# Moving weights by 512 columns instead of x by 256 in the FFNs and output projections of a four-layer float32 trunk

## What is computed

```python
for i in range(DEPTH):
    x = x + 0.5 * _swiglu(_rms_norm(x, norm_ffn1[i]), ffn1_w_gate[i], ffn1_w_up[i], ffn1_w_down[i])
    h = _rms_norm(x, norm_mix[i])
    ...          # y = fox mixer, conv module or diff mixer of h, each with an output projection
    x = x + y
    x = x + 0.5 * _swiglu(_rms_norm(x, norm_ffn2[i]), ffn2_w_gate[i], ffn2_w_up[i], ffn2_w_down[i])
```

## Time and profile before

| what | value |
|---|---|
| runs | 2136.51, 2139.57, 2136.52 us |
| median | 2136.52 us |
| span of the profiled execution, first to last instruction | 2137.5 us |
| own time of the profiled execution | not listed apart from its span |
| TensorE matmul busy | 2076.1 us, 97% |
| VectorE, ScalarE, GpSimd busy | 64%, 45%, 6% |
| mean granted TensorE clock | 0.992 of full |
| HBM read | 341.38 MB, 160 GB/s over the span |

### The profile page before, as it was taken

One profiled execution on the slowest core, in us unless ns is written; L12 is line 12 of the kernel. 1 busy time (PEld: TensorE's weight loads), 2 busy tenths in 40 slices (PEclk: granted clock), 3 DMA queues, 4 the chain that ended last, 5 costly groups with the idle time before them and its releaser, 6 DMA issues.

```text
span 2137.5 us, 39342 instructions
## 1 busy us (share of the span) xinstructions
PE 2076.1 (97%) x16546; PEld 2001.7 (94%) x16546; DVE 1377.3 (64%) x1532; ACT 960.1 (45%) x1057; POOL 124.8 (6%) x119
## 2 busy tenths in 40 slices
PE   7999999999999998899999999999999999999999
PEld 7999788999999997799999998799999999889999
DVE  6655767655755689565575558875557556776555
ACT  4435556334433440543453345564435435455442
POOL 2000301000200003100010000010001001101000
PEclk9999999999999999899999999999999999999999
DMA  6655333655455550165555554345555555434552
GB/s 198 198 184 178 119 118 119 197 184 189 150 186 186 167 178 8 59 208 179 178 177 192 182 175 139 118 138 182 190 178 178 180 191 161 122 117 159 189 184 98
DMA packets 261367, 343.73 MB, mean 161 GB/s; under 512 B 8086, under 2 KB 233887, under 8 KB 261279
## 3 DMA queue, kind: packets, MB, share of 16 engines
q1 hardware_dynamic: 261134, 342.41, 49.4%
q10 hardware_dynamic: 144, 0.05, 0.0%
HBM read 341.38 MB, written 1.05 MB: 160 GB/s over the span
## 4 chain that ended last, share of the span: by engine, by line
PE 86%; DVE 9%; issue 2%; ACT 2%; DMA 0%; DVEq 0%; POOL 0%; ACTq 0%; POOLq 0%
PE bank L1295 27%; PE bank L1297 26%; PE bank L1296 26%; DVE sb_w_low L735 3%; DVE sb_x_low L771 2%; PE bank L1427 2%; DVE sb_x_square L1182 2%; PE bank L1475 1%; DVE sb_xT L762 1%; PE bank L1442 1%; PE bank L1459 1%; PE bank L1430 1%; ACT sb_w_high L442 1%; PE bank L1573 0%; PE bank L1480 0%
## 5 line engine op out<-in xcount | busy, mean ns | idle before, releaser
L735 DVE TENSOR_TENSOR sb_w_low<-sb_raw,sb_w_high 128x2048 fp32r<-128x2048 f32 x324 | 757.1, 2337 | 449.9 <-ACT sb_w_high L442 448.9
L1295 PE MATMUL bank<-sb_x_high,sb_w_high 128*128 128x256 f32 x3328 | 950.9, 286 | 20.4 <-DVE sb_w_low L735 20.4
L1297 PE MATMUL bank<-sb_x_high,sb_w_low 128*128 128x256 f32 x3328 | 944.7, 284 | 0.0
L1296 PE MATMUL bank<-sb_x_low,sb_w_high 128*128 128x256 f32 x3328 | 944.4, 284 | 0.0
L442 ACT ACTIVATE sb_w_high<-sb_raw 128x2048 fp32r<-128x2048 f32 x324 | 616.7, 1904 | 178.5 <-PE bank L1297 178.4
L1295 PEld LDWEIGHTS bank<-sb_x_high,sb_w_high 128*128 128x128 f32 x3328 | 641.5, 193 | 27.9 <-DVE sb_w_low L735 24.1
L1296 PEld LDWEIGHTS bank<-sb_x_low,sb_w_high 128*128 128x128 f32 x3328 | 641.1, 193 | 1.5 <-issue 1.4
L1297 PEld LDWEIGHTS bank<-sb_x_high,sb_w_low 128*128 128x128 f32 x3328 | 640.9, 193 | 0.0
L1295 PE MATMUL bank<-sb_h_high,sb_w_high 128*128 128x256 f32 x1408 | 394.4, 280 | 0.0
L1296 PE MATMUL bank<-sb_h_low,sb_w_high 128*128 128x256 f32 x1408 | 392.8, 279 | 0.0
L1297 PE MATMUL bank<-sb_h_high,sb_w_low 128*128 128x256 f32 x1408 | 392.8, 279 | 0.0
(11 more groups left out here) (198 smaller groups left out, 1722.2 us busy)
## 6 DMA issues: line engine op xcount, KB each, us to landing
sb_raw<-in_ffn_w_gate SPq DMA_DIRECT2D x88, 1024.0 KB, 5.3
sb_raw<-in_ffn_w_up SPq DMA_DIRECT2D x88, 1024.0 KB, 5.3
sb_raw<-in_ffn_w_down SPq DMA_DIRECT2D x88, 1024.0 KB, 4.8
sb_raw<-in_fox_w_in SPq DMA_DIRECT2D x24, 1024.0 KB, 5.3
sb_raw<-in_conv_w_pw SPq DMA_DIRECT2D x12, 1024.0 KB, 5.4
sb_raw<-in_diff_w_in SPq DMA_DIRECT2D x12, 1024.0 KB, 5.0
sb_raw<-in_fox_w_out SPq DMA_DIRECT2D x8, 1024.0 KB, 4.8
sb_raw<-in_diff_w_out SPq DMA_DIRECT2D x4, 1024.0 KB, 4.8
```

The lines of the kernel that those rows point to most:

```text
L735: dve.tensor_tensor(w_low[b % RING][:, :], raw[b % RING][:, :], w_high[b % RING][:, :].bitcast(F32), ALU.subtract).then_inc(S["low_ready"], 1)
L1295: pe.matmul(dst, s_high, m_high, start=first, stop=False, skip_group_check=loose)
L1296: pe.matmul(dst, s_high, m_low, start=False, stop=False, skip_group_check=loose)
L1297: return pe.matmul(dst, s_low, m_high, start=False, stop=last, skip_group_check=loose)
```

## The change

x is now kept as `x_nat`, tokens on partitions (2 x 1024 values). In the FFNs and output projections x, h and o (128 tokens by 128 features) are the stationary operand, the weights the moving one with 512 columns: gate and up blocks lie in adjacent ring slots and are read as one operand, a down or output block is read in halves of 512 columns. A pair is then 72 matmuls of 512 columns and 4 transposes of the hidden tile, which now has tokens on partitions. The q, k and v products and conv's first projection keep 256 columns and need x with features on partitions, as x_high and x_low also do in gate and up; so at each boundary x is turned by 16 transposes (`turn_x`), in four parts.

The ring has 6 blocks; `raw` and `w_low` share memory, so that VectorE writes w_low over raw, and the load of block b waits until TensorE is done with block b-6. The gain is multiplied by VectorE out of PSUM (`gained`); the squares are summed by ScalarE along the free dimension (`accum_out`), and POOL's folds and the matmul of ones go. The inverse root has 2 columns, and is a per-partition factor in silu and in the gating; mixers get it as a row by a product with a diagonal (`inverse_row`). Loops over groups in the mixers are written out.

```diff
-RING = 3
+RING = 6
...
-        raw = [sb(f"raw{i}", [P, 2048]) for i in range(RING)]
-        w_high = [sb(f"w_high{i}", [P, 2048], F32R) for i in range(RING)]
-        w_low = [sb(f"w_low{i}", [P, 2048], F32R) for i in range(RING)]
+        with ExitStack() as landing:
+            raw = landing.enter_context(nc.sbuf_tensor("sb_raw", [P, RING, 2048], F32))
+        w_low = sb("w_low", [P, RING, 2048], F32R)
+        w_high = sb("w_high", [P, RING, 2048], F32R)
...
-                    sp.wait_ge(S["low_ready"], b - RING + 1 + u * per)
+                    sp.wait_ge(S["block_done"], done_at(b - RING) + 6 * u)
...
ScalarE, boundary
+                high(0)
+                high(1)
                 if i == 0:
...
+                square(0)
+                square(1)
+                high(2)
+                high(3)
+                act.wait_ge(S["square_ready"], 2 * i + 2)
                 if i:
                     act.wait_ge(S["inv_rms_ready"], i)
-                act.activation(root[:, 0:width], bank[7][:, 0:width], ACT.Sqrt, scale=1.0 / D, bias=eps[:, :]
+                act.activation(root[:, :], square_sum[:, :], ACT.Sqrt, scale=1.0 / D, bias=eps[:, :]
                                ).then_inc(S["root_ready"], 1)
...
ScalarE, a pair
                 def one_pair(p, u=0):
-                    split_high(b + 3 * p + 1, u, 6)
-                    silu(p, u)
-                    split_high(b + 3 * p + 2, u, 6)
+                    split_high(b + 3 * p + 2, u)
+                    if p == 0:
+                        act.wait_ge(S["inv_rms_ready"], i + 1)
+                    silu(p, 0, u)
+                    split_high(b + 3 * p + 3, u)
+                    silu(p, 1, u)
+                    split_high(b + 3 * p + 4, u)
                     high(p, u)
-                    split_high(b + 3 * p + 3, u, 6)
...
ScalarE, end of fox (diff and VectorE in the same way)
                     split_high(e + 4)
+                    split_high(e + 5)
                     o_part(g, 0)
...
VectorE, boundary
+                if i:
+                    update_x(i, 0)
+                    update_x(i, 1)
+                gained(0)
+                if i:
+                    update_x(i, 2)
+                low(0)
+                gained(1)
+                if i:
+                    update_x(i, 3)
+                else:
                     split_low(0)
+                    split_low(1)
+                low(1)
+                for j in (2, 3):
+                    gained(j)
+                    low(j)
...
VectorE, a pair
                 def one_pair(p, u=0):
+                    split_low(b + 3 * p + 2, u)
+                    if p == 0:
+                        inverse_rms(i)
+                    gated(p, 0, u)
+                    split_low(b + 3 * p + 3, u)
+                    gated(p, 1, u)
+                    if p == 0 and i == 0:
+                        before_tables()
+                    split_low(b + 3 * p + 4, u)
                     low(p, u)
...
TensorE
+            def rows_piece(b, piece, s_high, s_low, first, last, between=None):
+
+                high, low = (slot(t, b).rearrange("p (f n) -> p f n", f=2) for t in (w_high, w_low))
+                tt, half = x_parts[piece]
+                toks, cols = slice(tt * P, (tt + 1) * P), slice(half * HALF, (half + 1) * HALF)
+                for f in range(2):
+                    ins = three_passes(bank[piece][:, :], s_high[:, f, toks], s_low[:, f, toks],
+                                       high[:, f, cols], low[:, f, cols], first and f == 0, last and f == 1)
+                    if f == 0 and between:
+                        between()
+                return ins
...
+                def gate_up(p, tt, u=0, tiles=range(KT)):
...
+                    if tiles[0] == 0 and tt == 0:
+                        wait_block(blk + 1, u)
...
+                    for k in tiles:
+                        if p == 0 and k % 4 == 0:
+                            pe.wait_ge(S["xlow_ready"], 4 * i + 2 * tt + k // 4 + 1)
+                        ins = three_passes(pair(bank[4 + tt][:, :]), x_high[:, k, toks], x_low[:, k, toks],
+                                           high[:, :, k, :], low[:, :, k, :], k == 0, k == KT - 1)
...
+                def one_pair(p, u=0):
+                    gate_up(p, 0, u)
+                    gate_up(p, 1, u)
+                    turn_h(p, 0, u)
+                    down(p - 1, (0, 1), u)
+                    turn_h(p, 1, u)
+                    down(p - 1, (2, 3), u)
...
+                gate_up(0, 0, tiles=range(4))
+                turn_x(i, 2)
+                gate_up(0, 0, tiles=range(4, KT))
+                turn_x(i, 3)
+                gate_up(0, 1)
...
+                turn_h(0, 0)
+                gate_up(1, 0, tiles=range(4))
+                turn_h(0, 1)
+                gate_up(1, 0, tiles=range(4, KT))
+                gate_up(1, 1)
```

More of the change, by code:

```diff
@@ L215, in rows_of, with landed_at, phase_of, is_gate @@
             return v.rearrange("a (t p) -> (a t) p", p=P)
-        def raw_uses(b, u=0, per=0):
-            return 16 * (b // RING + 1) + u * (16 * per // RING)
+        def landed_at(b, u=0):
+            return 16 * (b // RING + 1) + u * 16
+        def phase_of(b):
+            return max(i for i in range(len(phases)) if starts[i] <= b)
+        def is_gate(b):
+            k = b - starts[phase_of(b)]
+            return phases[phase_of(b)] == "ffn" and (k == 0 or (k % 3 == 2 and k < 3 * PAIRS - 1))
+        def done_at(b):
+            return b + 2 if is_gate(b) else b + 1
+        def slot(t, b):
+            return t[:, b % RING, :]
+        def gate_columns(p, b):
+            gate = (b + 3 * p - 1 if p else b) % RING
+            return (0, 256) if gate < RING - 1 else (256, 0)
+        x_parts = [(0, 0), (0, 1), (1, 0), (1, 1)]
+        def x_part(t, j):
+            tt, kh = x_parts[j]
+            return t[:, 4 * kh:4 * kh + 4, tt * P:(tt + 1) * P]
         def pair(t):
@@ L645, in attention @@
                     fox_group(0)
-                    with act.Fori(0, GROUPS - 1) as u:
-                        fox_group(1, u)
+                    for j in range(1, GROUPS):
+                        fox_group(j)
                     exps(0, g, 0)
@@ L713, in conv @@
                                    ).then_inc(S["o_high_ready"], 1)
[L714 removed]
+                for k in range(3, 6):
                     split_high(e + k)
@@ L1400, in ffn @@
+                down(0, (0, 1), first=True)
+                turn_h(1, 1)
+                down(0, (2, 3), first=True)
                 one_pair(2)
```

644 lines of the change are left out of this document (303 added, 341 removed).

## The result

The changed kernel takes 2205.0 us, median of its four runs (2200.2, 2204.9, 2205.1 and 5192.5), against 2137.0 for the kernel before beside it: ratio 1.0309, 95% interval 1.0293 to 1.0325. The fourth was an execution in a slow state that the kernel before shows too (4037.7 us once); it is not in the ratio, and without it the median is 2204.9. The changed kernel is slower by 3.1%, where I had forecast 2117.5 us and given slower 24%. The profiled execution has a span of 2198.4 us, its mean granted clock 0.979 (before 0.992).

What follows compares the result with a forecast made beforehand. TensorE, busy 97% of the span, was taken as the bound. Terms -102 - 9 + 16 + 56 + 15 + 7 - 2 = -19 from 2137.5 gave a span of 2118.5, so 2117.5 us predicted; whole range 2055 to 2150.

Steps and rivals of the forecast that it cites:

- the spacing: FFN pairs and output projections: 512-column matmuls start every 215.8 ns, so a pair takes 16.01 us for 17.17, -102 us.
- the right upper bound, 226.6: Spacing of 512-column matmuls if a gate block's excess stays: 213.3 + 13.3 ns.
- the half-clock rows: TensorE after a fall to half clock: 213.8 ns per 256 columns, read as one column a cycle and no excess.
- Rival (a): All wide matmuls: the 13.3 ns excess stays as a fixed price, +73 us, 2190 us; chance 9%.
- The floor of 118 ns: TensorE: load and matmul together take at least about 118 ns; behind 213 ns of streaming the load is hidden.
- rival (d): TensorE streams more than one column a cycle, VectorE then bounds a pair at 8.6 us: 1466 us; chance 1%.
- The first pair: Start of each FFN: TensorE idles 7.0 us for 1.2, clock loses 1.5; 7.3 us eight times, +58.
- 15 + 7 - 9 and 5 of boundaries: Mixers: first blocks +15 us, ends +7, output projections -9, and part of the +16 for boundary transposes.
- the POOL term: FFN before conv: POOL's diagonal tiles slow VectorE's splits by 5 us; 2 us taken as gone.
- (b): FFN first pairs: little or no idle because the queues run ahead, 2049 us; chance 10%.
- (c): Steady FFN pairs wait for late blocks: 1 us late in each gives 2205 us, 0.3 gives 2144; chance 9%.
- (e): All wide matmuls: spacing per column unchanged, 236 ns for 512 columns, 134 us more, 2252 us; chance 3%.

Runs made afterwards that it cites:

- m1: Not a kernel version: reference work left out, streams of matmuls timed at rest and beside other engines; 512-column float32r 226.7 ns, 256-column 120 ns.
- e1: Changed kernel with root and two block splits moved earlier in the seven FFN phases behind another phase: 2143.8 us, ratio 1.0031.
- b4: b2 with one unused tile of 160 bytes ahead of the hidden and output tiles: 2117.4 us, ratio 0.9923 to the kernel before.
- m4: Reference work left out: streams at rest with stationary or moving tile shifted 0 to 256 bytes; 512 columns 226.7 to 237.3 ns.
- m5: Reference work left out: streams at rest with the two tiles' distance varied in 32-byte steps; 512 columns 226.7 to 234.2 ns.
- b2: Changed kernel with early root and splits in all FFN phases, mixers' edges reordered, hidden tile's turns joined: 2132.0 us, ratio 0.9976.
- e9: Kernel before, without the change, plus one unused tile of 32 bytes ahead of its tiles of x: 2122.9 us, ratio 0.9943.
- m2: Reference work left out: float32r streams at rest with transposes, a short matmul or a wait ahead of every 48; transient some 0.12 us.

## Why the prediction was wrong

**The step that failed is the spacing.** "A 512-column matmul should start every 215.8 ns." It is 226.7 in gate and up and 233.3 in the output pieces. In a pair that is 48 x 10.9 + 24 x 17.5 = 0.94 us, 83 us over 88 pairs, and 384 x 17.5 = 7 us in the output projections; the span missed by 79.9 in all, so the other terms together were 10 us too dear, 7 of them in the mixers. I had the right upper bound, 226.6, from a row of this very operation, and chose the other for a row that looked closer: the conv's, "the row that also has 512 cycles of stream and a load for each". That row is of plain float32, of which m1 shows 215.8 ns from record to record again; with float32r 13.3 ns come on top at 256, 384 and 512 columns, also when the same tile is loaded each time. What in the chip takes them is not shown. The type was the nearer likeness, not the cycles. The reading of the half-clock rows was right as a reading (213.8 for 256, and after 426.7 for 512, so one column a cycle and no excess), but it did not carry to 2.4 GHz, where there is an excess. Rival (a) is what happened, at 9%: its 2190 lacks the 6.7 ns of the output pieces (2496 matmuls, 17 us), and part of that is hidden by the terms that were too dear. My argument against it was the conv rows again; the one for it, "120 against 117.8 ns shows that something else than the load moves the spacing", was the trace's hint at the tiles' distance, and I read over it.

**The floor of 118 ns** ("what load and matmul together take at least") is near for 128 columns (113.6) and no proof for more: 256 columns also take 116.7 to 120. The step that nothing is left of it behind 213 ns of stream is what m1 refutes for float32r.

**More than one column a cycle**, rival (d), is refuted: nothing below 213 ns for 512 columns, bf16 included (213.5). The 131 ns of the Trainium skill (TensorE: Matmul & The Clock Gate, Back-to-back issue gap) do not hold here, for float32r (226.7) or for bf16.

**The first pair** was right in its mechanism and order: idle of some 6.3 us for 7.0 (from the starts; the two waits in the rows are 5.7), ended by `hidden` and then by `w_low`, with the clock at 1.2 GHz after it. The clock's loss was undersized: 13 matmuls at 426.7 ns lose 2.6 us, I had 1.5, from a fall behind a shorter idle. e1 prices the two at 7.9 us a phase; the forecast for them was 8.5 (the 7.3 is that less the 1.2 us of before). But I treated it as a cost of the change; it was a cost of the order of two queues, and went with no work taken away.

**The stages**, each from VectorE's first update of x to that of the next phase. An FFN of the changed kernel:

```profile
1108.05 0.69 DVE L732 SCALAR_TENSOR_TENSOR sb_x_nat<-bank,sb_x_nat 128x512 f32<-128x512 f32 x1 [2.25 <-PE bank L1271]
...
1305.81 0.69 DVE L732 SCALAR_TENSOR_TENSOR sb_x_nat<-bank,sb_x_nat 128x512 f32<-128x512 f32 x1 [2.25 <-PE bank L1271]
```

197.8 us (the others behind a phase 196.3 to 198.0) where I had 186.9: 11 pairs at 0.96 more make 10.6, so the boundary was priced right in sum, the idle a little too high and the clock too low. The mixers are longer by 1.1, 2.3, 6.9 and 7.6 us, 17.9 in all, for the 18 of my terms (15 + 7 - 9 and 5 of boundaries). That agreement is luck: the projections cost 7 us more than forecast, so first blocks and ends cost 7 less, at the first fox above all. How those split up is open. Of the POOL term (2 of 5 us taken as gone) nothing was to be seen in the changed kernel, whose FFN ahead of conv is 0.2 us longer than the next longest; the interference itself is there, and b4 shows it.

**Rivals (b), (c), (e).** (b) is what e1 makes of the kernel; in the kernel as changed the wait was there. (c) is refuted, steady pairs don't wait. (e), 236 ns for 512 columns, was nearer than my forecast for the output pieces (233), for a reason it did not name.

## What to carry to other kernels

Take the price of a matmul from a row of the same data type at the same clock; a stream of the same length in another type says nothing of its excess, and an excess that vanishes at half clock can be there at full. Halving the number of instructions gains only their fixed part, here 13 of 120 ns. When a change makes two waits into one at a phase's start, write both queues' new order before anything else: what waited was work that could have run while TensorE was covered. And where one operation shows two spacings in one kernel, look at where its tiles lie before looking at its neighbours. When a tile is moved, work out where all tiles behind it come to lie.

## What was not expected of the hardware

- A float32r matmul of 128 rows and 128 stationary columns costs its columns at 2.4 GHz plus 13.3 ns (226.7 for 512, 173.4 for 384, 120 for 256), whether its weight load brings another tile or the same one (m1), and with no regard to casts, subtractions or transfers beside it. bf16 has 0.2 to 2.5 ns (213.5, 109.2). At 1.2 GHz there is none (426.7). A matmul without a weight load was not measured.
- The distance of stationary and moving tile modulo 256 bytes moves it: 512 columns 226.7 at 0 and 229 to 237 elsewhere (m4, m5), 256 columns 120 at 0 and 116.7 to 119.6 elsewhere. In whole kernels one unused tile was worth 11 us of 2132 (b4 against b2) for 512 columns, and 12 of 2134 (e9) for 256, where 25 won over x and 8 lost over the hidden tile are in it. Why is open.
- 128 columns of float32r take 111 to 114 ns (m1, m4), hardly less than 256.
- Each short matmul or transpose put between dense stretches in m2 costs 0.06 to 0.09 us at its successor's start and up to 4 ns on each of some 11 behind it.
- VectorE's subtraction of two SBUF tiles took 3.69 us for 0.69 beside POOL's diagonal tiles, in the changed kernel and in b4.
